# Hybrid attention and RG-LRU block on one core: operand loads of the down projection moved ahead of stores, their splits two units later, partial outputs fetched early

## The reference

```python
def conv_gated_mlp(h, w_gate, w_up, conv_ffn_w, conv_ffn_b, w_down):
    g = causal_dwconv(h @ w_gate, conv_ffn_w, conv_ffn_b)
    return (jax.nn.gelu(g) * (h @ w_up)) @ w_down
...
        h = rmsnorm(x, norm_ffn_pre[l])
        y = conv_gated_mlp(h, w_gate[l], w_up[l], conv_ffn_w[l], conv_ffn_b[l], w_down[l])
        x = x + rmsnorm(y, norm_ffn_post[l])
```

## Time and profile before

| | before |
|---|---|
| median of three runs | 2195.97 us |
| the profiled execution, device time | 2196.11 us |
| its span | 2194.3 us |
| TensorE matmul busy | 2116.4 us (96%) |
| DVE busy | 1699.7 us (77%) |
| ACT busy | 1029.9 us (47%) |
| DMA mean rate | 193 GB/s |
| mean granted TensorE clock | 0.985 |

### The profile page before, as it was taken

How to read it: one execution, slowest core, us unless ns; L and a number is a source line. 1 busy time by engine, 2 the same in 40 slices (tenths; PEclk the granted TensorE clock), 3 DMA queues, 4 the chain that set the end, 5 groups by cost and what they waited for, 6 DMA issues and landing times.

```text
span 2194.3 us, 44374 instructions
## 1 busy us (share of the span) xinstructions
PE 2116.4 (96%) x18322; PEld 2096.3 (96%) x18322; DVE 1699.7 (77%) x2310; ACT 1029.9 (47%) x1293; POOL 346.9 (16%) x431
## 2 busy tenths in 40 slices
PE   9999999999999999999999999999977998998995
PEld 8999999999999999999999999999977998997995
DVE  7776777778755977888888888888867668667886
ACT  6555555447322654444444444444435445444442
POOL 0222222222100011121112111121211001003003
PEclk9999999999999999999999999999988999998998
DMA  5788888888533437888887888888776558669545
GB/s 174 184 197 192 201 205 203 179 205 175 159 111 97 161 121 210 216 222 219 216 219 214 221 213 222 218 224 220 210 195 226 164 177 263 170 164 281 170 136 173
DMA packets 238754, 423.84 MB, mean 193 GB/s; under 512 B 17008, under 2 KB 151792, under 8 KB 237312
## 3 DMA queue, kind: packets, MB, share of 16 engines
q1 hardware_dynamic: 147776, 256.84, 35.3%
q0 software_dynamic: 88224, 159.97, 35.1%
q10 hardware_dynamic: 2592, 4.72, 0.6%
HBM read 382.64 MB, written 89.16 MB: 215 GB/s over the span
## 4 chain that ended last, share of the span: by engine, by line
PE 85%; DVE 6%; issue 4%; DMA 2%; ACT 2%; POOL 1%; POOLq 0%; DVEq 0%; ACTq 0%
PE bank L2025 27%; PE bank L2026 27%; PE bank L2027 27%; DMA act_lo_f<-t_spill 2%; PE bank L2104 1%; PE bank L2117 1%; DVE w_all L1173 1%; DVE tsum L1844 0%; ACT w_all L724 0%; DVE act_lo L1844 0%; PE bank L2129 0%; PE bank L2128 0%; DVE w_all L1814 0%; ACT act_hi L1091 0%; PE bank L2189 0%
## 5 line engine op out<-in xcount | busy, mean ns | idle before, releaser
L2025 PE MATMUL bank<-act_hi,w_all 128*128 128x256 f32 x3312 | 922.4, 279 | 21.8 <-DVE up L1905 8.5
L2026 PE MATMUL bank<-act_lo,w_all 128*128 128x256 f32 x3312 | 916.8, 277 | 0.0
L2027 PE MATMUL bank<-act_hi,w_all 128*128 128x256 f32 x3312 | 916.7, 277 | 0.0
L2025 PEld LDWEIGHTS bank<-act_hi,w_all 128*128 128x128 f32 x3312 | 624.1, 188 | 27.8 <-DVE up L1905 8.7
L2026 PEld LDWEIGHTS bank<-act_lo,w_all 128*128 128x128 f32 x3312 | 624.1, 188 | 0.7 <-issue 0.2
L2027 PEld LDWEIGHTS bank<-act_hi,w_all 128*128 128x128 f32 x3312 | 624.0, 188 | 0.0
L2025 PE MATMUL bank<-tsum,w_all 128*128 128x256 f32 x1312 | 364.1, 277 | 11.5 <-DVE y_rest L1907 3.8
L2026 PE MATMUL bank<-tsum,w_all 128*128 128x256 f32 x1312 | 363.6, 277 | 0.0
L2027 PE MATMUL bank<-tsum,w_all 128*128 128x256 f32 x1312 | 363.6, 277 | 0.0
L1085 ACT ACTIVATE w_all<-raw_s 128x1024 fp32r<-128x1024 f32 x176 | 186.9, 1062 | 257.6 <-PE bank L2027 244.7
L1814 DVE TENSOR_TENSOR w_all<-raw_s,w_all 128x1024 fp32r<-128x1024 f32 x176 | 215.4, 1224 | 79.9 <-ACT w_all L1085 78.7
(11 more groups left out here) (382 smaller groups left out, 3463.0 us busy)
## 6 DMA issues: line engine op xcount, KB each, us to landing
raw<-weights SPq DMA_DIRECT2D x262, 512.0 KB, 4.3
w_sums<-weights POOLq DMA_DIRECT2D x96, 512.0 KB, 7.0
raw_s<-weights SPq DMA_DIRECT2D x84, 512.0 KB, 5.6
raw_s<-weights POOLq DMA_DIRECT2D x84, 512.0 KB, 5.9
raw_a<-weights SPq DMA_DIRECT2D x66, 512.0 KB, 5.4
raw_s<-w_sums SPq DMA_DIRECT2D x48, 512.0 KB, 5.0
t_spill<-h_out POOLq DMA_DIRECT2D x48, 256.0 KB, 3.7
act_lo_f<-t_spill POOLq DMA_DIRECT2D x11, 1024.0 KB, 9.6
```

What stands on the lines that cost most here:

```text
L2025: pe.matmul(dst, ah, bh, start=start, stop=False, skip_group_check=goes_on)
L2026: pe.matmul(dst, ah, bl, start=False, stop=False, skip_group_check=goes_on)
L2027: return pe.matmul(dst, al, bh, start=False, stop=stop, skip_group_check=goes_on)
```

## The change

The load of operand 0 of block 0 goes to iteration 36 of POOL's loop. In iteration 41 operands 1 and 2 are loaded ahead of the `store_t3` and 3 to 6 behind it. All splits of operands move: operand 0 of block 0 from k = -2 to k = -9, of the other blocks to k = 2, operands 1 to 6 from k = 5 to 10 to k = 7 to 12, and operand 6 of block 2 to k = 13. Four partial outputs are read back in iteration 54, four rounds before block 2, into four places that are free by then (`gb`, `cv`, `up`, half of `sq`), the other twelve in iteration 58; `Y_TILES` is reordered for this. The last part of the diff stands twice in the code, on ACT and on DVE. Nothing is computed otherwise, and no instruction on ACT, DVE or TensorE is added or taken away.

```diff
-T_AFTER = {1: 5, 2: 6, 3: 7, 4: 8, 5: 9, 6: 10}
+def t_turn(c, n):
+
+    if n == 0:
+        return 2 if c else -9
+    return 13 if n == 6 and c == CH - 1 else n + 6
...
-        Y_TILES = [t2_flat[:, S * t:S * t + S] for t in range(8)] + [
-            gb[:, 0:S], cv[:], up[:], h_out[:, 0], h_out[:, 1], y_rest[:], rms[:], sq[:, 0]]
+        Y_TILES = [gb[:, 0:S], cv[:], up[:], sq[:, 0]] + [t2_flat[:, S * t:S * t + S] for t in range(8)] + [
+            h_out[:, 0], h_out[:, 1], y_rest[:], rms[:]]
...
             def load_y(t):
-                if t < 4:
-                    pool.wait_ge(unit_used, N_FAST + 7 * (NS + 2 * PAIRS_OUT - 1) + 6)
-                    pool.wait_ge(y_stored[t // 2], 16 * PAIRS_OUT + 32)
-                if t == 4:
-                    pool.wait_ge(pu_done, NS + 2 * PAIRS_OUT + 1)
-                    for e in range(2):
-                        pool.wait_ge(y_stored[e], 32 * PAIRS_OUT)
                 pool.dma_start(Y_TILES[t], y_d[t]).then_inc(y_back[t // 2 % 2 if t < 4 else 0], 16)
+
+            def load_first_y():
+                pool.wait_ge(h_done, FT)
+                pool.wait_ge(tq_stored, 32 * HT)
+                pool.wait_ge(y_stored[0], 16 * PAIRS_OUT + 64)
+                pool.wait_ge(y_stored[1], 16 * PAIRS_OUT + 32)
+                for t in range(4):
+                    load_y(t)
+
+            def load_other_y():
+                pool.wait_ge(unit_used, N_FAST + 7 * (NS + 2 * PAIRS_OUT - 1) + 6)
+                pool.wait_ge(pu_done, NS + 2 * PAIRS_OUT + 1)
+                for e in range(2):
+                    pool.wait_ge(y_stored[e], 32 * PAIRS_OUT)
+                for t in range(4, KT):
+                    load_y(t)
...
             for i in range(NF):
-                if i <= NS:
+                c, o = (i + 1 - NS) // PAIRS_OUT, (i + 1 - NS) % PAIRS_OUT
+                if i == NS + PAIRS_OUT + 4:
+                    load_first_y()
+                if i > NS and i - 1 < NS + 2 * PAIRS_OUT:
+                    store_y(i - 1)
+                if i == NS - 6:
+                    load_t(0, 0)
+                if i >= NS and c + 1 < CH and o == PAIRS_OUT - 1:
+                    load_t(c + 1, 0)
+                if i >= NS - 1 and c < CH and o == 0:
+                    for n in range(1, 3):
+                        load_t(c, n)
+                    if i == NS - 1:
+                        store_after(PLAIN - 1 + i)
+                    for n in range(3, 7):
+                        load_t(c, n)
+                elif i <= NS:
                     store_after(PLAIN - 1 + i)
                 elif i == NS + 1:
                     store_t3(HT - 1)
...
-                c, o = (i + 1 - NS) // PAIRS_OUT, (i + 1 - NS) % PAIRS_OUT
-                if i > NS and i - 1 < NS + 2 * PAIRS_OUT:
-                    store_y(i - 1)
-                if i >= NS - 2 and c + 1 < CH and o == PAIRS_OUT - 1:
-                    load_t(c + 1, 0)
-                if i >= NS - 1 and c < CH and o == 0:
-                    for n in range(1, 6):
-                        load_t(c, n)
-                    if c == CH - 1:
-                        load_y(0)
-                        load_y(1)
-                    load_t(c, 6)
                 if i == NS + 2 * PAIRS_OUT:
-                    for t in range(2, KT):
-                        load_y(t)
+                    load_other_y()
...
-                k = 7 * (i - (NS - 1)) + n
                 for c in range(CH):
-                    if k == 7 * PAIRS_OUT * c - 2:
-                        convert(c, 0)
-                    for m in range(1, 7):
-                        if k == 7 * PAIRS_OUT * c + T_AFTER[m]:
+                    for m in range(7):
+                        if 7 * (i - (NS - 1 + PAIRS_OUT * c)) + n == t_turn(c, m):
                             convert(c, m)
```

## The result

| | before | after |
|---|---|---|
| median | 2197.76 us (4 runs, 2191.04 to 2199.97) | 2159.76 us (4 runs, 2159.03 to 2160.59) |
| ratio | | 0.9832, 95% interval 0.9809 to 0.9855 |
| span of the profiled execution | 2194.3 us | 2158.6 us |
| DVE busy | 1699.7 us | 1698.8 us |
| mean granted TensorE clock | 0.985 | 0.991 |

The change makes the kernel 1.7% faster; the forecast was 2159.3 us. The lines of the changed kernel stand about 12 further down: `first_of_b` is L1899 and L1907, `c22_of` L1917 and L1919, the matmuls L2037 to L2039.

The account below looks back on a forecast made before the run. TensorE was taken to wait for late DVE results, from landings and DVE's own work. Losses of 1.0 + 9.9 + 0.8 + 6.4 + 5.9 + 1 = 25.0 us replace 61.8: 2196.1 - 36.8 = 2159.3 us; 8 in 10: 2151 to 2174.

Parts of the forecast that it names:

- 61.8 us of loss: TensorE time lost between rounds 40 and 58 in gaps and slow clock, to become 25.0 us.
- the lateness of `first_of_b`: Down projection: DVE's queue of operand and weight splits makes this result 4.9, 3.2 and 4.3 us late in blocks 0 to 2.
- Operand 0 of block 0: Loading it four rounds early removes the 12.6 us gap and its 1.6 us of clock; 1.0 us stays.
- (d): Only operand 0 of block 0 pays, later positions give back the rest: 2182.7 us; chance 0.05 with cases near it.
- Block 0: DVE's queue up to c22_of is 9.9 us late in all, plus 0.8 for a possible half-clock stretch.
- Block 1: DVE's queue up to c22_of is 6.4 us late, in two gaps near 2.9 us at full clock.
- Block 2: 5.9 us late at c22_of, with first_of_b 4.3 late and a half-clock stretch of 1.6 inside.
- Landings: Operand loads arriving under DMA load in the three blocks: 1 us in all, since the rows have slack.
- the 7.2 us of round 58: Gap put down to operand 6 of block 2 landing behind partial outputs; to go, with 2.5 us of restart and clock.
- (a): Landings stay late in the blocks, 3 to 4 us each plus half-clock stretches: + 13, 2172 us; chance 0.19.
- (b): DVE's gaps shrink, least loss 22 us: 2156, or 2150 with 2 us less in each block; chance 0.10.
- (c): Weight loads through SP starve beside operand loads, slower: 2212 us at 40 us a load; chance 0.04 with no effect.

Follow-up runs that it names:

- the repeat: The changed kernel measured once more, unedited, five runs beside the kernel with the waiters first: 2161.14 us.
- the waiters first: Changed kernel with first_of_b put ahead of the fourth operand's low part on DVE, c22_of ahead of the sixth's: 2156.42 us, measured again 2156.06.
- the first experiment: Kernel before the change with only operand 0 of block 0 loaded in iteration 36 and split behind k = -9: 2182.19 us, ratio 0.9928.

## Why the prediction was right

**The bound and the loss.** 61.8 us of loss were to become 25.0; the trace has 25.0. DVE's queue was added up from its own rows, and the lateness of `first_of_b`, forecast at 4.9, 3.2 and 4.3 us, was 4.5, 3.0 and 4.1 (the distance of the two starts across the gap, less 0.113); in round 39 the gap is the 0.7. Doubling DVE's price cost 53 us, making the waited-for result go first took 2.2 us from each gap for `first_of_b`, moving the loads by 2.7 us changed these gaps by 0.04 at most. That DVE's queue sets the gaps is shown. After which gap the clock falls is not explained by any run.

**Operand 0 of block 0.** 13.4 us were forecast (2182.7 as rival (d)), 14.5 measured with this part alone (12.3 between the traced executions).

**Block by block.** Block 0: 9.9 and 0.8 for the clock, 10.0 measured; the stretch at 1.2 GHz lay between the gaps. Block 1: 6.4, 8.0 measured. This is the term that was too small: the row of a 2.8 us gap with full clock was taken to hold for both, and after the 2.86 us gap the clock fell, some 1.5 us. Block 2: 5.9 and 5.9. Landings: 1 us was put in, nothing found in the gaps. The errors of size (0.7 and 1 too much, 1.6 too little) cancel, so the closeness of 0.5 us is partly luck; the repeat gave 2161.1, and there block 0 lost 11.6 us and block 1 6.3.

**One step failed, without weight in the sum.** The prediction put the 7.2 us of round 58 down to operand 6 landing "behind partial outputs" and listed the early fetch as what keeps it away. The fetch is worth nothing (2160.6 with it undone), and with the fetch early but the split at its old turn the gap is 6.5 us. The load cannot start before round 57 ends, as the prediction's own working for block 2 has it (t = 19.3); the split at k = 13 is what removed the wait.

**The rivals.** (a), landings stay late: ACT waited for no operand in the blocks; loads a whole unit later brought no gap. (a)'s own sign, ACT waiting for operands, showed with the loads late and with the splits early, and only in the second did it cost. (b), at most 22 us of loss: not reached by this change; with the waiters first the kernel came to its upper end (2156.1 to 2156.4 against 2156). (c), weights starve: its sign was there, though the time was right. ACT waited for the weights of unit 4 once a block (2.5, 1.5 and 4.6 us). (c) had named weights 6, and its counter, that no weight split of ACT waits for a landing, was true of the kernel before only. DVE was further behind (in block 2 it takes these weights at 1986.67, 1.4 us after ACT is done with them), so nothing came on the path. (d) fell with the first experiment.

## What to carry to other kernels

Where an engine is the late one, add up its queue from the first delayed instruction to each result that another engine waits for; here that gave the lateness to 0.4 us, and it shows which result to move forward. A split or a wait belongs at the turn where its landing can be there: in block 2 moving the split took the wait away, and moving the transfers ahead of the load did nothing. Before work goes from DVE to POOL, see whether the DVE instructions beside it read two SBUF operands.

## What the runs showed of the hardware

A POOL instruction of 5.47 us on SBUF held a DVE instruction of 0.75 us for 5.02 us, and in the other two blocks one of 1.22 us for 5.56. That a 512 KB weight load from SP lands after 13.5 us in a block where it takes 4 to 6 us elsewhere was known from the trace before; new is that it reached ACT.

The length of a gap does not alone decide whether TensorE's clock falls behind it. In these traces, over rounds 39 to 58, no gap under 1.75 us was followed by a stretch at 1.2 GHz and every gap of 3.00 us or more was. Between, both occur: full clock after gaps of 2.82, 2.83 and 2.93 us, 1.2 GHz after 1.75, 1.79 and 2.41. The same kernel with the waiters first, run twice, shows both behind one gap of 1.75 us in block 2:

```profile
1980.30:1983.80 3.50, 3.50 (x18) 0.55 1.10 256
```

```profile
1978.60:1982.10 3.50, 2.94 (x24) 1.00 1.10 252
```

A stretch costs 1.1 to 2.9 us here, and the gap doesn't set that either: after 4.28 to 4.32 us it was 15 matmuls in one trace and 28 in another. Two traces whose gaps add up to nearly the same can differ by 3 to 4 us through this alone.
